# Two-bank element-wise operations for the heavy experts of a hybrid trunk on one core

## What is computed

```python
def swiglu(h, wg, wu, wd):
    return (jax.nn.silu(h @ wg) * (h @ wu)) @ wd

def moe_swiglu(h, router, eg, eu, ed):
    ...
    logits = (t @ router).astype(jnp.float32)
    top_v, top_i = lax.top_k(logits, TOP_K)        # 2 of 8 experts
    top_w = jax.nn.softmax(top_v, axis=-1)
    combine = jnp.sum(jax.nn.one_hot(top_i, N_EXPERTS, dtype=jnp.float32) * top_w[..., None], axis=1)
    out = jnp.zeros((b * s, d), jnp.float32)
    for e in range(N_EXPERTS):
        out = out + combine[:, e:e + 1] * swiglu(t, eg[e], eu[e], ed[e]).astype(jnp.float32)
    return out.astype(h.dtype).reshape(b, s, d)
```

## Time and profile before

| | |
|---|---|
| median of three runs | 1355.52 us (1355.41 to 1357.62) |
| the profiled execution | 1355.3 us |
| its span, first to last instruction | 1353.5 us |
| PE busy | 1320.2 us, 98% |
| DVE busy | 1120.3 us, 83% |
| ACT busy | 941.3 us, 70% |
| mean granted clock of PE | 0.993 of full speed |

### The profile page before, as it was taken

The page is one execution under the profiler, slowest core; times in us unless marked ns, Lnnn a source line. Parts: engine busy times, 40 slices in busy tenths (PEclk is TensorE's granted clock), DMA queues, the critical chain, the costliest instruction groups (busy, mean ns, idle before and its releaser), DMA issues.

```text
span 1353.5 us, 17501 instructions
## 1 busy us (share of the span) xinstructions
PE 1320.2 (98%) x6684; PEld 1098.8 (81%) x6685; DVE 1120.3 (83%) x1037; ACT 941.3 (70%) x879; POOL 104.2 (8%) x67
## 2 busy tenths in 40 slices
PE   8999999999999999999999999999999999999994
PEld 5898888887898878888888888887888888888873
DVE  5767655556766899999999999999999999999986
ACT  4644444444644778788787887887878787888774
POOL 1140000000231100100001001100000001000020
PEclk9999999999999999999999999999999999999998
DMA  9434655553523799999999999999999999999992
GB/s 354 183 108 161 232 187 186 186 199 113 186 97 138 303 365 378 410 404 420 410 402 421 415 414 403 416 420 375 416 418 404 420 399 410 415 421 419 407 420 92
DMA packets 63029, 437.47 MB, mean 323 GB/s; under 512 B 7231, under 2 KB 7409, under 8 KB 11746
## 3 DMA queue, kind: packets, MB, share of 16 engines
q1 hardware_dynamic: 58896, 423.23, 78.2%
q0 software_dynamic: 3904, 13.06, 2.6%
q10 hardware_dynamic: 146, 0.07, 0.0%
HBM read 430.04 MB, written 6.29 MB: 322 GB/s over the span
## 4 chain that ended last, share of the span: by engine, by line
PE 86%; DVE 8%; ACT 2%; DMA 2%; issue 1%; SPq 0%; DVEq 0%; ACTq 0%
PE ps L2118 34%; PE ps L2142 18%; PE ps L2238 8%; PE ps L1806 4%; DVE w_lo L405 4%; PE ps L2258 4%; PE ps L1821 4%; PE ps L1909 3%; PE ps L2247 2%; PE ps L1783 2%; DMA raw<-in_stream 2%; ACT w_hi L400 1%; PE ps L2134 1%; DVE spare_w L405 1%; PE ps L2178 1%
## 5 line engine op out<-in xcount | busy, mean ns | idle before, releaser
L405 DVE TENSOR_TENSOR w_lo<-raw,w_hi 128x2048 fp32r<-128x2048 f32 x313 | 715.2, 2303 | 125.8 <-ACT w_hi L400 124.8
L400 ACT ACTIVATE w_hi<-raw 128x2048 fp32r<-128x2048 f32 x315 | 600.1, 1917 | 163.6 <-PE ps L2118 67.6
L2118 PE MATMUL ps<-w_hi,xT_hi 128*128 128x512 f32 x564 | 224.3, 398 | 1.8 <-DVE xT_lo L1366 1.3
L2118 PE MATMUL ps<-w_lo,xT_hi 128*128 128x512 f32 x564 | 220.4, 391 | 0.0
L2118 PE MATMUL ps<-w_hi,xT_lo 128*128 128x512 f32 x564 | 219.7, 390 | 0.0
L405 DVE TENSOR_TENSOR spare_w<-raw,spare_w 128x2048 fp32r<-128x2048 f32 x85 | 194.5, 2288 | 10.0 <-ACT spare_w L400 9.5
L400 ACT ACTIVATE spare_w<-raw 128x2048 fp32r<-128x2048 f32 x85 | 163.1, 1918 | 18.7 <-PE ps L2142 16.1
L2118 PEld LDWEIGHTS ps<-w_hi,xT_hi 128*128 128x128 f32 x564 | 106.1, 188 | 23.0 <-DVE xT_lo L1366 1.5
L2118 PEld LDWEIGHTS ps<-w_lo,xT_hi 128*128 128x128 f32 x564 | 105.9, 188 | 22.8
L2118 PEld LDWEIGHTS ps<-w_hi,xT_lo 128*128 128x128 f32 x564 | 106.2, 188 | 20.8
L2142 PE MATMUL ps<-w_hi,aT_hi 128*128 128x512 f32 x288 | 114.1, 396 | 2.6 <-DVE w_lo L405 2.0
(11 more groups left out here) (352 smaller groups left out, 1983.4 us busy)
## 6 DMA issues: line engine op xcount, KB each, us to landing
raw<-in_stream SPq DMA_DIRECT2D x400, 1024.0 KB, 7.9
outs<-work POOLq DMA_DIRECT2D x5, 512.0 KB, 9.2
gain<-in_gains POOLq DMA_DIRECT2D x4, 512.0 KB, 5.3
h<-in_x SPq DMA_DIRECT2D x2, 512.0 KB, 6.7
raw<-in_stream SPq DMA_DIRECT2D x2, 512.0 KB, 6.4
tokens<-big POOLq DMA_DIRECT2D x2, 512.0 KB, 3.3
outs<-work POOLq DMA_DIRECT2D x4, 256.0 KB, 7.6
out<-work SPq DMA_DIRECT2D x4, 256.0 KB, 2.8
```

Of the source, the lines that this page charges most:

```text
L400: nc.scalar.activation(home(n, 0), raw[:, n % RAW, :], ACT.Copy).then_inc(hi_done, 1)
L405: nc.vector.tensor_tensor(home(n, 1), raw[:, n % RAW, :], home(n, 0).bitcast(F32), ALU.subtract).then_inc(lo_done, 1)
L2118: last = nc.tensor.matmul(ps[:, 4 + s, :], (xT_hi, xT_lo)[xp][:, k, x * P:(x + 1) * P], w((n + half), wp, kk * 512, (kk + 1) * 512), start ...
```

## The change

In steps with heavy double blocks the four pairs of element-wise operations become four single ones that cover both banks: `heavy_silu` and `heavy_mul` (banks 4 and 5), `heavy_aT` on ACT and on DVE (banks 6 and 7). The silu and the product of the first block leave their place ahead of unit `m+5`; both blocks are done behind unit `m+6`, after unit `m+3` has been used. The semaphores rise by two at once. PE's list is the same. On DVE the copy of the gathered rows moves ahead of unit `m+7`. In the last step the first light block's operations move ahead of the last unit, and two of the four `combine` to the end of the list.

```diff
+            def heavy_silu(n):
+
+                used(act, n)
+                nc.scalar.activation(gate_x[:, :, :], ps[:, 4:6, 0:FB], ACT.Silu).then_inc(fm.silu, 2)
+
+            def heavy_aT(B):
+
+                act.wait_ge(fm.aT_ps, B + 2)
+                copy(aT_hi[:, :, :, :].rearrange("p b f q -> p b (f q)"), ps[:, 6:8, 0:FB]).then_inc(fm.aT_hi, 2)
+
...
@@ -843,15 +853,12 @@
...
-                    ffn_aT(fm, 1, B, 0)
-                    ffn_aT(fm, 1, B + 1, 1)
+                    heavy_aT(B)
...
-                else:
-                    ffn_block(fm, 1, B + 2, 0, m + 2)
...
-                    ffn_block(fm, 1, B + 3, 1, m + 4)
+                    heavy_silu(m + 4)
...
@@ -1436,6 +1443,18 @@
...
+            def heavy_mul(B):
+
+                dve.wait_ge(fm.silu, B + 2)
+                nc.vector.tensor_tensor(act_x[:, :, :], gate_x[:, :, :], ps[:, 4:6, FB:2 * FB], ALU.mult).then_inc(fm.mul, 2)
+
+            def heavy_aT(B):
+
+                dve.wait_ge(fm.aT_hi, B + 2)
+                nc.vector.tensor_tensor(aT_lo[:, :, :, :].rearrange("p b f q -> p b (f q)"), ps[:, 6:8, 0:FB],
+                                        aT_hi[:, :, :, :].rearrange("p b f q -> p b (f q)").bitcast(F32),
+                                        ALU.subtract).then_inc(fm.aT_lo, 2)
+
...
@@ -1445,13 +1464,10 @@
...
-                    ffn_aT(fm, 1, B, 0)
-                    ffn_aT(fm, 1, B + 1, 1)
+                    heavy_aT(B)
...
-                if not next_light:
-                    ffn_block(fm, 1, B + 2, 0, m + 2)
...
@@ -1462,33 +1478,32 @@
                 lo_unit(dve, m + 5)
                 lo_unit(dve, m + 6)
                 if not next_light:
-                    ffn_block(fm, 1, B + 3, 1, m + 4)
+                    heavy_mul(B + 2)
...
-                if i == STEPS - 2:
-                    combine(0, 1)
-                    combine(1, 1)
-                lo_unit(dve, m + 7)
                 if i in TURN_AT:
                     p, g = TURN_AT[i]
                     if p < HEAVY:
                         gather_lo_heavy(p, g)
                     else:
                         gather_lo_light(p)
+                if ends:
+                    light_mul(B + 2, 0, 1)
+                    light_lo(B + 2, 0, 1)
+                lo_unit(dve, m + 7)
...
-                if ends:
-                    light_mul(B + 2, 0, 1)
-                else:
+                if not ends:
                     lo_unit(dve, m + 8)
                 if ends:
-                    light_lo(B + 2, 0, 1)
                     light_mul(B + 2, 1, 1)
                     light_lo(B + 2, 1, 1)
+                    combine(0, 1)
+                    combine(1, 1)
```

## The result

The changed kernel takes 1372.3 us (median of four runs, 1369.7 to 1374.7) against 1356.0 for the kernel before: a ratio of 1.0121, 95% interval 1.0106 to 1.0137, so 1.2% slower. The forecast was 1371.5 us, with a range of 1364.5 to 1378. The profiled execution took 1369.7 us, the lowest of the four, with a span of 1367.9.

The account below looks back on a forecast made before the run. PE's own list was taken as the clock of the experts. From the profiled 1355.3 us, +16.8 - 1.3 + 0.6 - 4.4 + 4.5 = +16.2 gave 1371.5 us, with a range of 1364.5 to 1378 us.

Parts of the forecast that it names:

- The step that carries it: At seven turns with a heavy double block next, PE's gather transposes wait for the merged product: +16.8 us in all.
- Part 1: Merged operations in heavy steps save some 0.15 us a pair, covered by PE: booked 0, at most 10 us.
- Part 3: DVE's copy of gathered rows, moved ahead of unit m+7, removes PE's 1.30 us wait at step 28: -1.3 us.
- Part 4: Small terms at four steps with a heavy block between light ones, at step 25 and at 478: together +0.6 us.
- the four tight steps: Steps with a heavy block between two light ones: +0.14 us each, four times, +0.6 us.
- the wait at 478: PE's wait of 0.46 us at 478 gets shorter as the product moved away: -0.3 us.
- Part 5: The last step: PE begins the last down product 4.9 us early, two `combine` hold DVE 0.5 us: -4.4 us.
- Part 6: PE's clock: 0 to 7 stretches at half clock, about 1.5 us lost each; three taken, +4.5 us.
- a count of six cases: Of six PE waits of about 1 us or more in the kernel before, three are followed by half clock.
- The second rival: The waits at the turns come but the clock stays: +11.7 us, 1367 us; chance 0.25.
- my slack: Unit m+10 has about 1 us of slack before a light double block, where a late gather could delay a split.

Follow-up runs that it names:

- experiment 1: The changed kernel with silu and product split in two again at the seven turns only, the first ahead of unit m+5: 1350.1 us, ratio 0.9959.
- experiment 4: The kernel before, with PE also waiting for the second block's product (bank 5) before the gather transposes at the seven turns: 1380.4 us, ratio 1.0183.
- experiment 5: The changed kernel with 20 idle matmuls on PE ahead of the gather's wait at the seven turns: 1367.1 us, ratio 1.0081.
- experiment 7: The kernel before with only DVE's new last step: 1350.9 us; the changed kernel with the old last step: 1378.4 us.
- 3: The changed kernel, at the seven turns with the gather behind the first down product and its copies behind unit m+7's split: 1351.0 us, ratio 0.9959.
- Experiment 6: The kernel before with one more DVE operation of 128 x 512 behind unit m+3's split in 34 heavy steps: 1366.1 us, ratio 1.0069.
- experiment 2: The changed kernel with the gather's transposes behind the first down product on PE at the seven turns: 1360.8 us, ratio 1.0034.

## Why the prediction was right

The step that carries it was right in place and size: the transposes wait for a product that now stands behind unit m+6. Worked out were 16.8 us, the positions give 2.34, 2.44, 2.44, 2.35, 2.71, 2.44 and 2.34, together 17.1. At steps 23 and 43 the product does come 0.2 us earlier than the old second one, as the first silu is gone from ACT's list; step 28 I had 0.3 too low. There the split of unit m+6 is late itself: ACT starts it at 930.28, 1.95 us ahead of the last matmul's start at 932.23, where it was 2.24 us at step 38 of this kernel and at step 28 of the kernel before. What holds it I did not test. Experiments 1, 4 and 5 tie the cost to it from three sides.

Part 1, nothing for the merge, holds: DVE's busy time fell by 2.7 us, about a quarter of the 10 us that Part 1 allowed it at most, and the time by none (experiment 1). The row from which I took 0.68 us for 512 columns gave the merged product to the digit. The Trainium skill's rule on rotating through PSUM banks (Perfetto Trace Analysis, section Matmuls) spoke against the edit. The trace agrees: 16.2 us of waits where there were none.

Part 3: the wait of 1.30 is gone. By positions that is worth 1.57 us (experiment 1), 0.3 more than booked, since the idle time of a record counts from the modelled end of the matmul before; it cancels the 0.3 that step 28 cost above the sum. Part 4 was 0.6 and came to 1.0: the four tight steps paid 0.17 to 0.21 instead of 0.14, and the wait at 478 shrank by 0.06, not by 0.33; why it did not shrink more I did not test. Part 5: -4.65 in the profile against -4.4, -4.6 in the medians of experiment 7; PE's last product came 4.8 us early against 4.9. The two `combine` held the next DVE operation as said: it starts at 1354.86, 2.1 us behind PE's 1352.76 where 1.84 was usual, 0.3 instead of 0.5.

Part 6, the clock, was a choice between bounds, three falls and 4.5 us. This profile has three, 4.6 us. The medians give 5.2 (experiment 5), experiment 4 shows five falls. The number came out, but it rested on little more than a count of six cases, so that it came out so closely is luck. What the prediction saw in those six, small products beside the three waits with a fall, does not part them from the others: in the kernel before four transposes stand right in front of the wait of 1.30 us too, and behind it the clock stayed at 1.00:

```profile
923.22 0.60 PE L2134 MATMUL ps<-cst,act_x 128*128 128x128 f32 x4
925.12 0.50 PE L2118 MATMUL ps<-w_hi,xT_hi 128*128 128x512 f32 x1 [1.30 <-DVE xT_lo L1366]
```

It is also the term that varies from run to run: 1369.7 to 1374.7 with waits, 1366.5 to 1368.4 without falls behind the turns. The second rival, waits without a price in clock, fell: by the sum it would have been 1367.0 (the 1366.5 that the prediction gives in one place is a slip), and experiment 5, in which no turn has a fall, gave 1367.1. The Trainium skill (TensorE: Matmul & The Clock Gate, Why this matters for your kernels) asks only that PE's idle gaps between bursts of matmuls stay below about 3 us. That is not enough here: gaps of 2.3 to 2.6 us were followed by half clock in three of seven cases, gaps of 2.1 to 2.3 us in five of seven.

The profile of the kernel before has slow stretches at 444 and 1297 that the one of after has not, 2.9 us; without them the spans would differ by 17.3, not 14.4. The one at 444, ahead of the experts, comes and goes in kernels of either kind (experiments 1 and 5 have it, 3 and 4 have not) and is not of the change. The one at 1297 stands in two profiles only, of the kernel before and of it with the new last step; whether it has to do with the change is not shown. The sum knew of neither, and part of its closeness to the median, 0.8 us, is luck.

Wrong was my slack: I wrote that unit m+10 has about 1 us before a light double block. Experiment 6 puts it at 0.2. It did no harm, since at the turns PE's wait moves the whole step with it; it did harm in experiment 2, where I took PE's wait away and left ACT's queue as it was.

## What to carry to other kernels

Before two operations are made one, ask who else waits for the earlier of them: here a gather of four or eight transposes that used its bank, not the main chain, and it cost 2.4 us seven times, while the merge saved time on engines that nobody waited for. Where a wait can't be avoided, move the waiting piece behind other work on the other queues that take part too, not on PE alone. And in a kernel like this one, where PE's list is the clock, price such a wait above its length: here 17.1 us of waits brought 5.2 us of slow clock with them.

## What the runs showed of the hardware

Whether a wait of the same length and with the same neighbours costs clock varies. Of seven like waits of 2.3 to 2.6 us three were followed by a stretch at 1.2 GHz in the changed kernel, and the same three when it ran with the old last step. In experiment 4, with waits of 2.1 to 2.3 us, it was five of seven; where 20 matmuls of 128 x 256 filled the waits, it was none. One such stretch cost 1.46 to 1.65 us by positions. I had not expected more falls behind the shorter waits, and no run here shows what decides.
